# The modulation sums of a conditioned decoder step: one unit of outputs for each column group, one turn for each set

## The reference

```python
# conditioning: one row for the prompt, eight for the samples (9 rows c)
m = silu(c) @ w_ada + b_ada            # (9, 6*1024): shift1, scale1, gate1, shift2, scale2, gate2
h = rmsnorm(x, norm1_w) * (1 + scale1) + shift1
z, xbc, dt, u, gates = split(h @ w_in)
ya = ssd_branch(z, xbc, dt, ...)       # causal conv, Mamba-2 scan, gated norm, @ w_out_a
yb = s5_branch(u, ...)                 # complex diagonal scan, gelu, GLU
x  = x + gate1 * ((sig(g0) * ya + sig(g1) * yb) @ w_out)
h  = rmsnorm(x, norm2_w) * (1 + scale2) + shift2
x  = x + gate2 * moe(h)                # 16 experts, top 2 inside the best of 4 groups
y  = rmsnorm(x, final_norm_w)
```

## Time and profile before

| | |
|---|---|
| median of 3 runs | 682.55 (682.54 to 683.07) |
| profiled execution, its own time | 683.83 |
| its span, first to last instruction | 681.7 |
| busy: PE, PEld | 626.8 (92%), 384.2 (56%) |
| busy: DVE, ACT, POOL | 360.5 (53%), 149.8 (22%), 138.8 (20%) |
| mean granted clock of TensorE | 0.957 of 2.4 GHz |
| weight matmuls of the units (128x512 moving, 32 columns of weights) | x192 records, 26.0 busy |
| folds (128x9 moving) | x96 records (80 + 16), 13.0 busy |
| `ada_copy` on VectorE | x8, 5.5 busy, 686 ns each |
| read from HBM | 170.56 MB, 261 GB/s over the span |

### The profile page before, as it was taken

One profiled execution on the slowest core, in us unless ns is written; L12 is line 12 of the kernel. 1 busy time (PEld: TensorE's weight loads), 2 busy tenths in 40 slices (PEclk: granted clock), 3 DMA queues, 4 the chain that ended last, 5 costly groups with the idle time before them and its releaser, 6 DMA issues. The chain is left out here.

```text
span 681.7 us, 8960 instructions
## 1 busy us (share of the span) xinstructions
PE 626.8 (92%) x3363; PEld 384.2 (56%) x3363; DVE 360.5 (53%) x940; ACT 149.8 (22%) x301; POOL 138.8 (20%) x237
## 2 busy tenths in 40 slices
PE   3889999999999999999799997689999999998994
PEld 2367777676767777665567774533434434344343
DVE  3896975888988634688872224612314224122036
ACT  3532434301000241322310011511111011010104
POOL 2200120499889115003000002100000000000000
PEclk9789997999999999999999999579999999998997
DMA  8989733033333270599968934389999999999931
GB/s 262 389 221 368 251 123 131 3 124 124 123 125 124 59 227 1 207 387 348 294 200 304 391 124 180 148 331 425 431 417 430 428 422 429 427 422 429 429 144 72
DMA packets 64380, 178.55 MB, mean 262 GB/s; under 512 B 9828, under 2 KB 27956, under 8 KB 58192
## 3 DMA queue, kind: packets, MB, share of 16 engines
q1 hardware_dynamic: 60788, 170.57, 65.7%
q0 software_dynamic: 1296, 4.72, 1.8%
q10 hardware_dynamic: 2252, 2.67, 1.3%
HBM read 170.56 MB, written 7.39 MB: 261 GB/s over the span
## 5 line engine op out<-in xcount | busy, mean ns | idle before, releaser
L666 PE MATMUL psum<-projection_region,ring 128*128 128x288 f32 x768 | 197.1, 415 | 4.1 <-DVE projection_region L1608 2.6
L666 PEld LDWEIGHTS psum<-projection_region,ring 128*128 128x128 f32 x768 | 146.9, 194 | 50.9 <-issue 10.3
L666 PE MATMUL psum<-ring,gate_region 128*64 128x512 f32 x400 | 107.5, 608 | 2.1 <-DMA mixer_region<-in_w 1.4
L1608 DVE TENSOR_TENSOR gate_region<-gate_region,psum 128x288 f32<-128x288 f32 (+1 forms) x16 | 12.0, 749 | 170.6 <-PE psum L666 148.6
L1287 ACT ACTIVATE gate_region<-psum 128x512 f32<-128x512 f32 (+2 forms) x65 | 35.8, 564 | 275.8 <-PE psum L666 173.3
L666 PE MATMUL psum<-mixer_region,gate_region 128*64 128x512 f32 x256 | 77.8, 594 | 0.0
L666 PEld LDWEIGHTS psum<-ring,gate_region 128*64 128x64 f32 x400 | 33.9, 140 | 69.9 <-issue 68.6
L1614 DVE SCALAR_TENSOR_TENSOR x_features<-psum,modulation,x_features 128x256 f32<-128x256 f32 x72 | 34.1, 473 | 27.8 <-PE psum L666 27.8
L666 PEld LDWEIGHTS psum<-mixer_region,gate_region 128*64 128x64 f32 x256 | 24.2, 137 | 22.1 <-issue 21.7
L650 POOL TENSOR_TENSOR gate_region<-group_key 128x1 f32<-128x1 f32 x8 | 1.8, 230 | 163.1 <-DVE gate_region L2176 157.5
L666 PE MATMUL psum<-gate_region 128*128 128x288 f32 x128 | 34.8, 415 | 0.0
(11 more groups left out here) (270 smaller groups left out, 812.3 us busy)
## 6 DMA issues: line engine op xcount, KB each, us to landing
ring<-in_w SPq DMA_DIRECT2D x25, 2048.0 KB, 22.5
mixer_region<-in_w SPq DMA_DIRECT2D x15, 2048.0 KB, 25.5
ring<-in_w_ada SPq DMA_DIRECT2D x12, 2048.0 KB, 11.0
ring<-in_w_in SPq DMA_DIRECT2D x10, 2048.0 KB, 11.6
projection_region<-in_w SPq DMA_DIRECT2D x4, 2048.0 KB, 22.7
tok_region<-in_w SPq DMA_DIRECT2D x4, 1536.0 KB, 25.2
ring<-in_w_glu SPq DMA_DIRECT2D x2, 2048.0 KB, 7.7
ring<-in_w_out_a SPq DMA_DIRECT2D x2, 2048.0 KB, 11.5
```

The source lines that it names most:

```text
L666: return nc.tensor.matmul(out, lhsT, rhs, start=first, stop=last, skip_group_check=True)
L1608: return v.tensor_tensor(out, x, y, op)
```

## The change

The outputs go in sets: two sets of four units (units 0 to 3, 4 to 7) and two of two (8 and 9, 10 and 11). In a set of four, column group c takes the outputs of unit c, over all 1024 rows; the bank adds up over the set's four DMAs. A DMA is still 2 MB, but holds 256 rows of 2048 columns in place of 1024 rows of 512 (in a set of two, 512 rows of 1024 columns; two column groups then share a unit's outputs, each with half of the rows). A set is copied once, turned once by four transposes, and added once (sets of two: two linked adds, as two partial sums are left). The set's first unit waits for the add of the set before (`mod_ok`). The copy of set 0 stays on ScalarE, those of sets 1, 2 and 3 on VectorE. Sets 1 and 2 are copied in the second half of rounds 1 and 2 and turned at their ends. Set 3 is `ada(10)` and `ada(11)` in their old places and is copied where unit 11 was; its turn moves from between the token rows' transposes to behind the second slot list, its add behind the count of passes, and the experts wait for it. Square sums of the second norm group go to bank 4, as bank 5 holds set 3.

```diff
-        ada_odd = part(xbc_r, 0, 512)
...
+        def set_bank(s):
+            return (5, 6, 6, 5)[s]
+        def set_sums(s):
+            sums = ps[:, set_bank(s), :].rearrange("p (c g r) -> p g c r", c=4, g=4)
+            return [sums[:, :, :, 0:NC]] if s < 2 else [sums[:, q::2, :, 0:NC] for q in range(2)]
...
                 if n < 4:
-                    return a["w_ada"][0, :, n * 512:(n + 1) * 512], KD
+                    return a["w_ada"][0, 256 * n:256 * (n + 1), 0:2048], 2
...
-                    i = n - U_ADA2 + 4
-                    return a["w_ada"][0, :, i * 512:(i + 1) * 512], KD
+                    i = n - U_ADA2
+                    if i < 4:
+                        return a["w_ada"][0, 256 * i:256 * (i + 1), 2048:4096], 2
+                    if i < 6:
+                        return a["w_ada"][0, 512 * (i - 4):512 * (i - 3), 4096:5120], 4
+                    return a["w_ada"][0, 0:512, 5120:6144], 4
...
             def ada(i):
+                s, t, k = (i // 4, i % 4, 2) if i < 8 else (i // 2 - 2, i % 2, 4)
...
-                if i >= 4:
-                    pe.wait_ge(ada_cp, i)
-                elif i == 3:
-                    pe.wait_ge(x_ok, KD)
+                if t == 0 and s:
+                    pe.wait_ge(mod_ok, s)
                 for r in range(2):
                     for c in range(4):
-                        last = mm(ps[32 * c:32 * c + 32, sums_bank(i), :], cT[:, 4 * r + c, :], w[:, 4 * r + c, :], r == 0, r == 1)
+                        kk, u = (r, c) if k == 2 else (2 * (c % 2) + r, c // 2)
+                        last = mm(ps[32 * c:32 * c + 32, set_bank(s), :], cT[:, k * t + kk, :], w[:, kk, 512 * u:512 * (u + 1)],
+                                  t == 0 and r == 0, t == 8 // k - 1 and r == 1)
...
+            def ada_turn(s):
+                pe.wait_ge(ada_cp, s + 1)
                 for c in range(4):
-                    last = mm(turned(i, c, c + 1), ada_sum(i)[:, c * P:(c + 1) * P], sel9[:, 0:NC], c == 0, c == 3)
+                    last = tr(ps[:, set_bank(s), c * P:(c + 1) * P], ada_s[:, c * P:(c + 1) * P])
...
             ada(1)
+            ada(2)
+            ada(3)
+            pe.wait_ge(par_ok, 1)
             ada_turn(0)
-            ada(2)
-            ada_turn(1)
-            ada(3)
-            ada_turn(2)
-            ada_turn(3)
...
-                    pe.wait_ge(mod_ok, (4, 5, 6, 7, 8, 9, 10, 10)[hp])
...
                 if units:
                     ada(units[1])
-                    ada_turn(units[0])
...
-                if units:
-                    ada_turn(units[1])
+                if qd in (1, 2):
+                    ada_turn(qd)
...
-            square_sums(5, 4, 8)
+            square_sums(4, 4, 8)
...
-                if j == 0:
-                    ada_turn(10)
-                elif j == 2:
+                if j == 2:
...
-            ada_turn(11)
             pe.wait_ge(h_ok, 2)
             h2_turn(0, 2)
+            pe.wait_ge(ada_cp, 4)
             h2_turn(1, 2)
...
             slot_list(1)
+            ada_turn(3)
...
             gathered_turn(0)
+            pe.wait_ge(mod_ok, 4)
...
-            sum_copy(0)
             rsqrt(n1v, n1y)
-            for i in range(1, 4):
-                sum_copy(i)
+            act.wait_ge(unit_used, ada_unit(3) + 1)
+            f(ada_s[:, :], ps[:, set_bank(0), :]).then_inc(ada_cp, 1)
...
-                units = UNITS_OF[qd]
-                if units:
-                    ada_copy(units[0])
...
-                if units:
-                    ada_add(units[0])
-                    ada_copy(units[1])
+                if qd in (1, 2):
+                    ada_copy(qd)
...
-                if units:
-                    ada_add(units[1])
+                if qd in (1, 2):
+                    ada_add(qd)
...
-            ada_copy(10)
-            dve.wait_ge(mod_ok, 10)
+            dve.wait_ge(mod_ok, 3)
             scales(nw2, 32)
...
-            ada_copy(11)
+            ada_copy(3)
...
-            ada_add(11)
...
             dve.wait_ge(route_ok, 1)
+            ada_add(3)
```

More of the change, by code:

```diff
@@ L401, in weights @@
                     return a["w_out"][0, :, (n - U_OUT) * 512:(n - U_OUT + 1) * 512], KD
-                return a["w_ada"][0, :, 11 * 512:12 * 512], KD
+                return a["w_ada"][0, 512:1024, 5120:6144], 4
             def load(out, in_, s):
@@ L1021, in _ @@
                     ada(units[1])
-                    ada_turn(units[0])
                 else:
                     pe.wait_ge(xs_ok, 5)
-                    pe.wait_ge(ada_cp, 10)
+                    pe.wait_ge(mod_ok, 3)
                     mm(ps[:, 6, 0:T], ones[:], sq_acc, True, True).then_inc(g0_ps, 1)
@@ L1653, in norm_scale, with ada_copy, ada_add @@
                 norm_refine(vv, y, t, n)
-            def ada_copy(i):
-                dve.wait_ge(unit_used, ada_unit(i) + 1)
-                dve.wait_ge(adaT_ps, i)
-                if i == 4:
+            def ada_copy(s):
+                dve.wait_ge(unit_used, ada_unit((3, 7, 9, 11)[s]) + 1)
+                dve.wait_ge(adaT_ps, s)
+                if s == 1:
                     dve.wait_ge(st_s5, 64)
-                v.tensor_copy(ada_s[:, :], ps[:, sums_bank(i), :]).then_inc(ada_cp, 1)
-            def ada_add(i):
-                dve.wait_ge(adaT_ps, i + 1)
-                tt(mod[:, 4 * i:4 * i + 4, :], turned(i, 0, 4).rearrange("p (k c) -> p k c", c=NC),
-                   b_ada[:, 4 * i:4 * i + 4].unsqueeze(2).to_broadcast([P, 4, NC]), ALU.add).then_inc(mod_ok, 1)
+                v.tensor_copy(ada_s[:, :], ps[:, set_bank(s), :]).then_inc(ada_cp, 1)
+            def ada_add(s):
+                dve.wait_ge(adaT_ps, s + 1)
+                m0, n = (16 * s, 4) if s < 2 else (16 + 8 * s, 2)
+                sums = set_sums(s)
+                mv = mod[:, m0:m0 + 4 * n, :].rearrange("p (g c) r -> p g c r", c=4)
+                bias = b_ada[:, m0:m0 + 4 * n].rearrange("p (g c) -> p g c", c=4).unsqueeze(3).to_broadcast([P, n, 4, NC])
+                last = tt(mv, sums[0], bias, ALU.add)
+                if s >= 2:
+                    link(last)
+                    last = tt(mv, mv, sums[1], ALU.add)
+                last.then_inc(mod_ok, 1)
             def per_sequence(col):
@@ L1751, in _ @@
             level(2)
-            dve.wait_ge(adaT_ps, 3)
-            tt(mod[:, 0:12, :], ps[:, 6, 0:12 * NC].rearrange("p (k c) -> p k c", c=NC),
-               b_ada[:, 0:12].unsqueeze(2).to_broadcast([P, 12, NC]), ALU.add).then_inc(mod_ok, 3)
             rotated(8, 3, 0, 0)
-            ada_add(3)
-            dve.wait_ge(mod_ok, 4)
+            ada_add(0)
+            dve.wait_ge(mod_ok, 1)
             scales(nw1, 8)
@@ L2018, in _ @@
                 decayed(2 * qd + 1)
-                if units:
-                    ada_add(units[0])
-                    ada_copy(units[1])
-                else:
+                if qd in (1, 2):
+                    ada_copy(qd)
+                elif qd == 3:
                     dve.wait_ge(g0_ps, 2)
@@ L2034, in _ @@
             dve.wait_ge(sq_used, 12)
-            norm_var(5, D // G, nv)
+            norm_var(4, D // G, nv)
             group_normed(1)
-            ada_copy(10)
-            dve.wait_ge(mod_ok, 10)
+            dve.wait_ge(mod_ok, 3)
             scales(nw2, 32)
@@ L2048, in _ @@
                 tt(gates[:, j, :], gates[:, j, :], gates[:, KD + j, :], ALU.add).then_inc(mrg_ok, 1)
-                if j == 0:
-                    ada_add(10)
             def residual(j, src, gate, done):
@@ L2200, in add_up @@
                     dve.wait_ge(x1_ok, KD)
-                    dve.wait_ge(mod_ok, 12)
+                    dve.wait_ge(mod_ok, 4)
                 else:
```

18 lines of the change are left out of this document (1 added, 17 removed).

## The result

The changed kernel took 678.42 us (median of 20 runs, 675.79 to 681.98), the kernel before 683.36 (20 runs beside it, 681.54 to 687.53): ratio 0.9925, 95% interval 0.9908 to 0.9942, which is 5.1 us, or 4.0 to 6.3. The profiled execution of the kernel after took 678.29 (span 676.2); before, 683.83 (span 681.7).

A forecast was written before the change was run, and what follows sets the result against it. A chain of waits bounds the kernel: savings ahead of the gather at 440.14 show one for one in the end. 0.2 + 3.78 + 0.89 + 1.56 = 6.43 us, from 682.55 to 676.1; range 674.0 to 679.4.

The forecast's parts named there:

- Quads: Quads 0 to 2: copies, adds and folds removed, saving 1.34, 1.22 and 1.22 us, sum 3.78; bounds 2.1 and 4.5.
- level queues: Quads 0 to 2: TensorE and VectorE alternate in ending last, so the later one decides each quad's gain.
- third term: Quad 2: VectorE gains 0.71 from a copy and an add, plus its 0.51 stall, 1.22 us.
- First stage: Up to 40 us: first tile 0.57 earlier, low clock takes back 0.2 to 0.5; 0.2 us taken, bounds -0.3 and 0.57.
- state loads: Quad 3: state tile 7's transposes come 2.8 us late if nothing moves; two covers hide it, cost 0 to 1.5, taken 0.
- second cover: Units loaded in rows of 4 or 8 KB instead of 2 KB transfer faster, at best 1.9 us earlier.
- rival 3: Quads: more holes in TensorE's queue lower its clock, kernel slower; one whole quad low costs 13 us, 689; chance 0.07.
- Projection: First projection after the mixer: unit 10's fold leaves TensorE's path, 0.89 us; bounds 0.6 and 1.2.
- Router: Router: unit 11's fold no longer delays the positions VectorE waits for, 1.56 us; bounds 1.2 and 1.6.
- named signs of failure: State-load wait, clock below 1.00 between 281 and 343, VectorE's off-term stall unchanged, or gather released by the token store.
- The list stays last: Router: GpSimd's gather still waits last for the list, as the tokens' second store moves up by the same 1.56 us.
- likeliest case: Whole kernel: the forecast itself, 674.9 to 677.5 us, with chance 0.60.

The follow-up runs named there:

- copies_quads: Changed kernel with VectorE's four removed copies back in quads 0 to 2, results unused; quads took 15.11, 15.14 and 16.06 us (14.33, 14.55, 15.94 without).
- folds_mid: Changed kernel with four fold-like TensorE matmuls back in the middle of quads 0 to 2, results unused; quads took 15.32, 15.40 and 16.10 us.
- router_only: Kernel before with only the last unit's turn moved behind the second slot list and its add behind the passes' count, fold kept; ratio 0.9995.
- after_again: The changed kernel run again with no edit; ratio to the kernel before 0.9917.
- unit0_short: Changed kernel with the first modulation unit loaded by four DMAs in rows of 2 KB again; ratio to the kernel before 0.9904.
- short_rows: Changed kernel with the seven units of the second and third set loaded in rows of 2 KB again; quad 3's stretch took 16.45 us.
- fill_right: Changed kernel with unused matmuls, sized to TensorE's idle time, added from the first stage to the router to hold its clock; ratio 0.9873.

## Why the prediction was right, and where it was not

**Quads.** Forecast 1.34, 1.22, 1.22; measured 1.48, 1.30, 0.81, sum 3.59 against 3.78. The mechanism, level queues, is shown by copies_quads and folds_mid for quads 0 and 1. In quad 2 it does not hold: VectorE is late there by itself, and the third term was mis-sized. I priced VectorE's copy at its start-to-start time and did not look at GpSimd's sums beside it, which make the following multiply 0.49 longer.

**First stage.** From the sum of squares to the first tile 1.00 came in the profiled execution and 0.5 in most others (0.57 was forecast; the other 0.5 is the matmuls of that sum, at the low clock in the kernel before and nearly at the full one in this execution after), and the clock took back from -0.2 to +1.0 more than before in the tile's 64 matmuls (0.2 to 0.5). Near nothing, as the 0.2 said, against the one profiled execution of the kernel before that the forecast had; against router_only, which has the same code there and waited 2.65 for folds, it is 1.4 to 2.6 from the sum of squares through the 64 matmuls. What failed is a term that is not there: I gave longer rows only a possible gain, for the state loads, and none of their effect on the small parameter loads at the very start, 1.06 to 1.4 on the path.

**Quad 3.** The state loads cost nothing, as taken; without the second cover their transposes came 0.94 late, not the 2.8 that I had, so ScalarE's wait covered them alone. The low clock in the profiled execution (1.62) is rival 3 in small; since it also fell on unchanged code and stayed away in after_again, unit0_short, copies_quads and short_rows, the change is not shown to cause it.

**Projection.** Forecast 0.89. Where quad 3 ran at full clock the stretch went from 14.98 to 14.02: 0.96. The 1.29 of the profiled execution has part of quad 3's loss in its start.

**Router.** Forecast 1.56, measured 1.9 to 2.4 in the ten executions without filling there. The positions came 1.81 earlier and VectorE's wait went down by 2.05. Of the named signs of failure two came: a granted clock below 1.00 between 281 and 343 (0.52 in quad 3), and here the gather's releaser, which is the store of the tokens. "The list stays last" was wrong, since the list gained more than the second store (10.84 behind the turn instead of 11.83), and 0.7 of the list's gain ends there. That this term reaches the end of the kernel rests on the traces and the sum below; the kernel that has it alone did not show it in its time.

**Sum.** Forecast 6.4; start -1.1 to -1.4, first stage about 0, quads 3.6, projection 0.96, router 2.2: 5.4 to 5.7, against 5.1 (4.0 to 6.3) measured. The direction held, and the time lies in the range, though above the likeliest case of 674.9 to 677.5. Of the miss of 2.3 us 0.8 is the base, three runs that were faster than the twenty; the rest, 1.3 to 1.5, is about what the parameters behind the first unit's long rows cost. That the sum came so near is in part luck: quad 2 gave 0.4 less than forecast, and the router 0.6 more.

## What to carry to other kernels

When a DMA's rows are made longer, look at who shares the DMA engines with it: small loads in another queue come later, and at the start of a kernel that is on the path. An operation taken off VectorE is worth its time only if what moves into its place does not meet GpSimd there; here a copy from PSUM stood in that shadow for free (0.69). And where the time goes with the granted clock, read stages from the trace at full clock, and count what TensorE's new idle time costs as a chance, not as a fixed term.

## What the runs showed of the hardware

A 128x128 matmul with 128 columns in f32 is two passes of 0.12, 0.23 together, at the full clock; a transpose of that size is one, 0.13 to 0.15. GpSimd's 128x288 product takes 0.67 or, beside VectorE's operations on SBUF alone, 1.53, and those, of 128x1024, go from 1.22 to 1.68. From the issue of the tokens' last store (128 KB, behind 1 MB of others) to GpSimd's release by it took 2.8 to 3.0 in the nine executions with the same order of stores and no filling there, and 3.5, 3.9 (with the 1 MB in two stores) and 4.7 with matmuls filling TensorE, with the DMA engines idle by 434 in the last case, 1.8 before GpSimd was released; no run here says why. The granted clock fell to 0.50 in the router with TensorE busy throughout (fill_right, 427.5 to 430.5); what lets it fall there is open.
